# Gate columns of the Fourier and pooling branches as seven block products for eight, in the first mixing stage

## The reference, cut to what matters

```
h = rmsnorm(x, g_mix[l])
p = h @ w_in[l]                       # 1024 -> 512 F, 512 B, 512 C, 512 V, 512 P, 3 * 1024 gates
gates = sigmoid(p[..., OFF_G:])       # 0: Fourier, 1: convolution, 2: pooling
y_f = fourier_mix(p[F], w_fourier[l])           # FFT over tokens and channels, 128 x 256 maps
y_c = short_conv(p[B], p[C], p[V], w_conv[l], w_conv_out[l])
y_p = pool_mix(p[P], w_pool[l], pool_scale[l])
merged = gates0 * y_f + gates1 * y_c + gates2 * y_p
x = x + merged @ w_o[l]
```

## Time and profile before

| | before |
|---|---|
| median of three runs | 2216.32 us |
| profiled execution's own time | 2219.73 us |
| its span, first to last instruction | 2217.9 us |
| TensorE busy | 2208.1 us |
| VectorE busy | 1729.5 us |
| ScalarE busy | 1320.1 us |
| mean granted TensorE clock | 0.999 |

### The profile page before, as it was taken

How to read it: one execution, slowest core, us unless ns; L and a number is a source line. 1 busy time by engine, 2 the same in 40 slices (tenths; PEclk the granted TensorE clock), 3 DMA queues, 4 the chain that set the end, 5 groups by cost and what they waited for, 6 DMA issues and landing times.

```text
span 2217.9 us, 28791 instructions
## 1 busy us (share of the span) xinstructions
PE 2208.1 (100%) x11494; PEld 1886.3 (85%) x11494; DVE 1729.5 (78%) x2163; ACT 1320.1 (60%) x1489; POOL 56.2 (3%) x68
## 2 busy tenths in 40 slices
PE   9999999999999999999999999999999999999999
PEld 8888888888888888888888888888888888788887
DVE  7787566888788566788887799768788887976787
ACT  6565445556556544666656676555565667754554
POOL 0000000000000000000000000000000000000000
PEclk9999999999999999999999999999999999999999
DMA  8987555977879555698597753549778785345876
GB/s 278 312 233 260 166 186 188 311 224 232 287 245 275 182 173 207 221 300 234 193 319 232 238 171 113 203 162 326 229 235 277 239 259 196 107 162 195 283 247 185
DMA packets 170950, 503.86 MB, mean 227 GB/s; under 512 B 18720, under 2 KB 23328, under 8 KB 162624
## 3 DMA queue, kind: packets, MB, share of 16 engines
q1 hardware_dynamic: 161456, 434.90, 55.1%
q0 software_dynamic: 9216, 67.11, 15.5%
q10 hardware_dynamic: 144, 0.00, 0.0%
HBM read 500.91 MB, written 1.05 MB: 226 GB/s over the span
## 4 chain that ended last, share of the span: by engine, by line
PE 94%; DVE 2%; DMA 2%; ACT 1%; issue 0%; SPq 0%; ACTq 0%; DVEq 0%
PE psum L756 25%; PE psum L757 13%; PE psum L692 12%; PE psum L694 12%; PE psum L693 12%; PE psum L887 4%; PE psum L891 4%; PE psum L889 4%; PE psum L724 2%; PE psum L767 1%; DMA raw<-t_gate_up_1a_dram 1%; DVE split_w L1842 1%; PE psum L1114 1%; PE psum L775 1%; DMA raw<-w_a_alone_dram 0%
## 5 line engine op out<-in xcount | busy, mean ns | idle before, releaser
L1842 DVE TENSOR_TENSOR split_w<-raw,split_w 128x2048 fp32r<-128x2048 f32 (+3 forms) x389 | 842.5, 2177 | 149.1 <-ACT split_w L1314 146.8
L1314 ACT ACTIVATE split_w<-raw 128x2048 fp32r<-128x2048 f32 (+3 forms) x389 | 708.0, 1829 | 290.9 <-PE psum L694 61.8
L756 PE MATMUL psum<-xt,split_w 128*128 128x512 f32 x2464 | 860.1, 393 | 2.5 <-DVE xt L1864 2.5
L757 PE MATMUL psum<-xt,split_w 128*128 128x256 f32 x2464 | 689.8, 280 | 0.0
L756 PEld LDWEIGHTS psum<-xt,split_w 128*128 128x128 f32 x2464 | 462.0, 187 | 105.8 <-DVE xt L1864 2.8
L757 PEld LDWEIGHTS psum<-xt,split_w 128*128 128x128 f32 x2464 | 466.1, 189 | 0.5
L692 PE MATMUL psum<-split_w,xt 128*128 128x512 f32 (+1 forms) x736 | 289.5, 393 | 0.0
L694 PE MATMUL psum<-split_w,xt 128*128 128x512 f32 (+1 forms) x736 | 283.7, 385 | 0.0
L693 PE MATMUL psum<-split_w,xt 128*128 128x512 f32 (+1 forms) x736 | 283.6, 385 | 0.0
L1980 DVE TENSOR_TENSOR gate_up<-psum,low 128x512 f32<-128x512 f32 x176 | 120.8, 686 | 99.4 <-ACT low L1391 99.3
L692 PEld LDWEIGHTS psum<-split_w,xt 128*128 128x128 f32 x736 | 138.4, 188 | 29.0 <-issue 3.0
(11 more groups left out here) (309 smaller groups left out, 2870.8 us busy)
## 6 DMA issues: line engine op xcount, KB each, us to landing
raw<-w_in_dram SPq DMA_DIRECT2D x180, 512.0 KB, 4.5
raw<-t_gate_up_1b_dram SPq DMA_DIRECT2D x88, 512.0 KB, 6.4
raw<-t_gate_up_2a_dram SPq DMA_DIRECT2D x88, 512.0 KB, 6.1
raw<-t_gate_up_2b_dram SPq DMA_DIRECT2D x88, 512.0 KB, 6.1
raw<-t_gate_up_1a_dram SPq DMA_DIRECT2D x84, 512.0 KB, 6.9
left_sums<-ffn_w_down_quarters_dram POOLq DMA_DIRECT2D x24, 1024.0 KB, 10.4
raw<-ffn_w_down_quarters_dram SPq DMA_DIRECT2D x48, 512.0 KB, 4.3
left_sums<-w_a_quarters_dram POOLq DMA_DIRECT2D x12, 1024.0 KB, 10.8
```

Source lines behind the costliest of these rows:

```text
L756: nc.tensor.matmul(bank, whi[:, slot, w], xt[:, c, :, :], start=c == 0, stop=False)
L757: last = nc.tensor.matmul(bank[:, 0:T], wlo[:, slot, w], xt_hi[:, c, :], start=False, stop=c == DC - 1)
L1314: nc.scalar.activation(whi[:, e.unit(u) % HL, 0:n], raw[:, r, 0:n], ACT.Copy).then_inc(hi_done, 1)
L1842: nc.vector.tensor_tensor(wlo[:, e.unit(u) % HL, 0:n], raw[:, r, 0:n], whi[:, e.unit(u) % HL, 0:n], ALU.subtract).then_inc(w_ready, 1)
```

## The change

With the tokens in halves, the rows of k in odd and even chunks and the two branches' 512 columns as the two column blocks, the gate columns of the Fourier and the pooling branch of one n are one 2 x 2 by 2 x 2 block product. Eight block products (four units of 24 matmuls, 96 in all) become seven (seven units of 12, 84 in all), in the order "11", "U", "T2", "21", "T3", "22", "T4". Three of them ("11", "21", "22") take quarters as they are loaded from `w_in`, four take sums of quarters; the sums are made by VectorE, in `gate_left` (U = 11 + 12, then + 22, then + 21) and in place in the slot of "12" (T3 = 12 + 22). The load of "22" waits for U; the next unit's load waits for T4. A turn is now 12 units for 9: seven products, f (the Fourier map), p (the pooling map), two units of convolution gates, here c0 and c1, and co (`w_conv_out`). The stage has 38 units for 32.

TensorE collects "11", "T2", "T3", "T4" in one bank and "U", "22" in another; ScalarE copies the intermediate contents out to `sigs` (`snapshot`) before the next product is added, and VectorE adds or subtracts (`x00`, `x11`, `x01`) before the Sigmoids. The sums of the tokens' halves are made once a stage by VectorE (`token_sums`, `token_sums_lo`) and ScalarE. Some work changes place in VectorE's order: the convolution (`convolved`) now stands behind the split of c0, and `bz_rounded` behind the split of co.

```diff
+GATES = (10, 22)
+GATE_ORDER = ("11", "U", "T2", "21", "T3", "22", "T4")
+GATE_SUMS = {GATES[n] + GATE_ORDER.index(name): (n, name) for n in range(2) for name in ("U", "T2", "T4")}
+MIX_UNITS = {1: 38, 2: 36}
...
 # SyncE's queue
+                    for name, q in (("11", "11"), ("21", "21"), ("T3", "12")):
+                        gate_load(u0 + gate_unit(n, name), q, n)
+                    eng.wait_ge(gate_sums, 4 * gate_turn(e, n) + 1)
+                    gate_load(u0 + gate_unit(n, "22"), "22", n)
+                    eng.wait_ge(gate_sums, 4 * gate_turn(e, n) + 4)
...
 # TensorE
+                    product(n, "11")
+                    if n == 0:
+                        eng.wait_ge(acted, e.after(acted, ("tok", "B")))
+                        eng.wait_ge(acted, e.after(acted, ("zt", 1)))
+                        turns("bt", tok)
+                        eng.wait_ge(done, e.after(done, ("s",)))
+                    product(n, "U")
+                    eng.wait_ge(acted, e.after(acted, ("e1", n)))
+                    product(n, "T2")
+                    if n == 1:
+                        eng.wait_ge(acted, e.after(acted, ("sig", 0, "c")))
+                    product(n, "21")
+                    eng.wait_ge(acted, e.after(acted, ("e2", n)))
+                    product(n, "T3")
+                    eng.wait_ge(acted, e.after(acted, ("u", n)))
+                    product(n, "22")
+                    eng.wait_ge(acted, e.after(acted, ("e3", n)))
+                    product(n, "T4")
...
 # ScalarE
+                gate_sum_split(0, "U")
...
+                gate_sum_split(0, "T2")
+                to_sbuf(("tok", "B"), tok, 2, u0 + 9)
                 split(u0 + 13)
...
+                    snapshot("e1", "11", sigs[:, 0, 0, :])
+                    gate_sum_split(n, "T3")
+                    snapshot("u", "U", sigs[:, 1, 1, :])
+                    split(u + 5)
+                    snapshot("e2", "T2", sigs[:, 1, 0, :])
+                    gate_sum_split(n, "T4")
+                    eng.wait_ge(done, e.after(done, ("wf", n)))
+                    split(u + 7)
+                    snapshot("e3", "T3", sigs[:, 0, 1, :])
...
 # VectorE (after z; before, split(u0 + 10) stood ahead of z)
+                split(u0 + 10)
+                gate_sum(0, "U")
+                gate_sum_split(0, "U")
+                gate_sum(0, "T2")
+                gate_sum(0, "T3")
+                gate_sum_split(0, "T2")
+                gate_sum(0, "T4")
+                split(u0 + 13)
+                for n in range(2):
+                    split(u + 4)
+                    split(u + 5)
+                    x00; gate_sum_split(n, "T4"); fourier_weights(n); split(u + 7); x11; split(u + 8); x01
+                    split(u + 9)
+                    if n == 0:
+                        convolved()
+                    else:
+                        for j in range(2):
+                            turned_lo(mt1_hi, mt1_lo, ("mt0", j), 6 + j, 2 * j)
+                    merge(0, "f", 4, sigs[:, 0, :, :])
+                    split(u + 10)
+                    merge(1, "p", 2 * (1 - n), sigs[:, 1, :, :])
+                    split(u + 11)
+                    if n == 0:
+                        bz_rounded()
+                    split(u + 12)
+                    if n == 0:
+                        gate_sum(1, "U"); gate_sum_split(1, "U"); gate_sum(1, "T2"); gate_sum(1, "T3")
+                        gate_sum_split(1, "T2"); gate_sum(1, "T4")
+                    else:
+                        split(u + 13)
+                    merge(2, "c", 4, sig1)
+                    split(u + (15 if n == 0 else 14))
```

More of the change, by code:

```diff
@@ L404, in build @@
         taken = semaphore("taken")
+        gate_sums = semaphore("gate_sums")
         small = signal("small")
@@ L552, in ffn_loads, with gate_load @@
                         down_load(u0 + 2 * FG + i, part, w2)
+            def gate_load(u, q, n):
+                load(u, [(chunked(1024 * j, 2, 512), gate_quarter(e, q, n, j)) for j in range(2)])
             def mix1_loads(u0):
@@ L993, in mix1_tensor @@
                 turns("zt", z)
[L994 to L1026, removed]
@@ L1027, in mix1_tensor, with left, product @@
-                u += 3
-                eng.wait_ge(acted, e.after(acted, ("sig", 1, "f")))
-                wide(u, 0, XT)
+                wide(u, 2, XT, 1, 4)
+                def left(name, i):
+                    if name in SUMMED:
+                        return [w[:, i, SUMMED[name], :] for w in (s_hi, s_lo)]
+                    c, m = {"11": (2 * i + 1, 0), "21": (2 * i, 0), "T4": (2 * i, 1)}[name]
+                    return [w[:, c, m * P:(m + 1) * P] for w in XT]
+                def product(n, name):
+                    out = psum[:, bank_of(n, name), :]
+                    u = u0 + gate_unit(n, name)
+                    slot = e.unit(u) % HL
+                    eng.wait_ge(w_ready, units(e, u, RAW))
+                    for i in range(DC // 2):
+                        hi, lo = left(name, i)
+                        w = slice(i * 512, (i + 1) * 512)
+                        start = i == 0 and name in ("11", "U", "21")
+                        stop = i == DC // 2 - 1
+                        nc.tensor.matmul(out, hi, whi[:, slot, w], start=start, stop=False, skip_group_check=True)
+                        nc.tensor.matmul(out, hi, wlo[:, slot, w], start=False, stop=False, skip_group_check=True)
+                        last = nc.tensor.matmul(out, lo, whi[:, slot, w], start=False, stop=stop, skip_group_check=True)
+                    last.then_inc(w_used, 1)
@@ L1030, in mix1_tensor @@
+                u = u0 + GATES[1] + 12
+                eng.wait_ge(done, e.after(done, ("mt0", 1)))
                 eng.wait_ge(done, e.after(done, ("merged", 1, "p")))
[L1031 to L1035, removed]
                 wide(u, 0, MERGED, 0, 1)
@@ L1539, in mix1_scalar @@
-                split(u0 + 14)
-                s = 12
-                for n in range(2):
[L1542 to L1561, removed]
@@ L2208, in mix1_vector @@
[L2208 to L2213, removed]
-                                                  psum[:, 6 + j, :].rearrange("p (c t) -> p c t", c=2),
-                                                  cv[:, 2 * j:2 * j + 2, :], ALU.mult).then_inc(
-                                                      done, e.mark(done, ("bc", j)))
@@ L2257, in mix1_vector @@
-                        s += 3
+                    split(u + 4)
+                    split(u + 5)
+                    multiplied(u + 3)
+                    eng.wait_ge(acted, e.after(acted, ("e1", n)))
+                    nc.vector.tensor_tensor(sigs[:, 0, 0, :], psum[:, bank_of(n, "21"), :], sigs[:, 0, 0, :],
+                                            ALU.add).then_inc(done, e.mark(done, ("x00", n)))
+                    gate_sum_split(n, "T4")
+                    fourier_weights(n)
+                    split(u + 7)
@@ new lines, in mix1_vector @@
+                    eng.wait_ge(acted, e.after(acted, ("e3", n)))
+                    nc.vector.tensor_tensor(sigs[:, 1, 1, :], sigs[:, 1, 1, :], sigs[:, 0, 1, :],
+                                            ALU.subtract).then_inc(done, e.mark(done, ("x11", n)))
+                    split(u + 8)
+                    multiplied(u + 5)
+                    nc.vector.tensor_tensor(sigs[:, 1, 0, :], psum[:, bank_of(n, "22"), :], sigs[:, 1, 0, :],
+                                            ALU.subtract).then_inc(done, e.mark(done, ("x01", n)))
@@ new lines, in mix1_vector @@
+                    split(u + 9)
+                    if n == 0:
+                        convolved()
+                    else:
+                        for j in range(2):
+                            turned_lo(mt1_hi, mt1_lo, ("mt0", j), 6 + j, 2 * j)
+                    multiplied(u + 7)
+                    eng.wait_ge(acted, e.after(acted, ("sig", n, "f")))
+                    merge(0, "f", 4, sigs[:, 0, :, :])
+                    split(u + 10)
+                    multiplied(u + 8)
+                    eng.wait_ge(acted, e.after(acted, ("sig", n, "p")))
```

275 lines of the change are left out of this document (198 added, 77 removed).

## The result

The changed kernel takes 2268.64 us (median of four runs, 2267.92 to 2269.33), the kernel before 2216.7 (2216.0 to 2217.28): 1.0231 times as long, interval 1.0218 to 1.0244.

The account below looks back on a forecast made before the run. TensorE was taken to bound the kernel before, VectorE's work and order the changed stretch. 2216.3 + 40.2 for two layers' stalls + 0.8 for the clock = 2257.3 us (forecast chance 0.78), range 2240 to 2270.

Parts of the forecast that it names:

- TensorE's saving: Mixing stages: 12 matmuls fewer per turn, 24 per layer at 0.227 us, 5.45 us a layer, 10.9 in two.
- A sum takes 2.29 us: VectorE's 128 x 2048 weight sums: priced like a split, 2.21 us behind another, 2.29 to the semaphore; eight per layer, 17.7.
- The token sums: Stage's start: about 4.9 us and later 2.2 on VectorE, 1.8 on ScalarE, costed at nothing; uncovered, up to 7 us.
- a load lands 4.75 us after the first issue: Weight loads in the mixing turns: one landing time for all; 3.8 us makes it 17.5 a layer, 5.5 us 23.1.
- The clock: TensorE's slow stretches after gaps longer than 2.5 us: 0.4 us a layer added, bounds 0 and 5.
- The chain's 20.1: VectorE's order followed from z to `w_o`: stalls 24.5, less 5.45, plus restarts, 20.1 us later per layer.
- The upper end of the forecast's own range: Whole kernel: loads landing in 5.5 us with the clock's upper bound, 2271 us.
- the list of what would show it: Expected profile signs: TensorE waits 20 to 25 us per layer behind VectorE's low parts, longest 4 to 5; `w_o` 20 later.
- VectorE's busy share: Sign in the first layer's stretch: VectorE busy over 85% from 243 to 357 us.
- Rival B: Mixing stretch: VectorE's throughput alone counts, 15.9 us of idle times don't arise, 4.2 a layer, 2225 us; chance 0.09.
- Rival A: Mixing stretch: VectorE's added work all hidden, TensorE alone counts, 2205.4 us, faster; chance 0.04.
- Rival C: Mixing stretch: TensorE's clock stays at its lower level until `w_o`, 16 to 55 us more a layer, 2290 to 2365; chance 0.05.

Follow-up runs that it names:

- the convolution's place: Changed kernel with the convolution moved on VectorE from ahead of merge f and c1's split to behind them, first turn: 2268.3 us, 1.0227 of the kernel before.
- mt0's 3.4 per layer: Changed kernel with `mt0`'s low halves moved on VectorE from ahead of merge f to behind c1's split, second turn: 2259.1 us.
- B's copy: Changed kernel with `mt0`'s low halves behind c1's split and, on ScalarE, the `tok` copy ahead of T2's copy in the first turn: 2257.7 us.
- the experiment: Changed kernel with loads of gate quarters, c0, c1 and co cut to 128 of each 512 columns: 2253.6 us, 1.0163 of the kernel before.

## Why the prediction was right, and where its size was off

**Right.** TensorE's saving (48 matmuls) and the mechanism: the low parts of U, T2, "21", c0 and c1 come late since VectorE has more work in the stretch than TensorE leaves time for. A sum takes 2.29 us to its semaphore, as taken. The token sums are hidden. By hand the low part of c1 began 43.6 us after z and its memsets; in the trace it is 284.72 - 239.85 = 44.9. The same chain, followed again before the experiments, foretold that the convolution's place is worth nothing, mt0's 3.4 per layer (measured 4.9 and 6.1), and B's copy next to nothing. That the time lies inside the range is in part luck: the size was 11 us short, both terms that were too small erred the same way, and 1.4 us more would have been outside.

**The loads, mis-sized.** The term "a load lands 4.75 us after the first issue" was too small. Loads with no other beside them took 5.15 and 5.17, c1's 5.2, and co's, issued 1.2 us behind c1's, 7.1. The range that I gave to this term (3.8 to 5.5) held the first three and not the last. The chain had one number for every load, from a median of the old order, where `w_conv_out` took 4.1. How much of the 5.2 and 5.6 us missing per layer this is, lies between the 3 of the rows and the 4 to 5 of the experiment.

**The clock, slightly mis-sized.** 0.4 us a layer was forecast, 1.0 and 2.4 measured, inside the bounds of 0 and 5. Not foreseen was that a gap of 2 us can be enough: the clock fell behind 1.96 us at U of the first layer. It is no fixed length, for it stayed at its upper level behind 2.11 us at the second layer's U, and behind 2.60 us in the kernel with sums of 64 columns. The gap and the clock behind it (2 us from 306 and from 862), first and second layer:

```profile
305.36 0.50 PE L1048 MATMUL psum<-split_w,mt_hi 128*128 128x512 f32 x1 [1.96 <-DVE split_w L1962]
...
860.60 0.50 PE L1048 MATMUL psum<-split_w,mt_hi 128*128 128x512 f32 x1 [2.11 <-DVE split_w L1962]
```
```profile
306.00:308.00 2.00, 2.00 (x6) 1.59 (x5) 1.77 (x1) 0.00 (x0) 0.00 (x0) 0.50 0.00 0
...
862.00:864.00 2.00, 1.66 (x8) 1.01 (x6) 2.00 (x2) 0.34 (x1) 0.00 (x0) 1.00 0.00 0
```

In all the clock is at its lower level for a quarter of the stretch in the first layer and a fifth in the second (1 - 0.88 = 0.12 and 1 - 0.90 = 0.10, twice that). That so much slow time costs so little was argued rightly: it ends in the next wait. The chain's 20.1, 3 to 5 for the loads and 1.0 to 2.4 for the clock make 24 to 27.5 for the 25.7 and 26.1 measured. Some 0.9 us by which the low part of c1 came late (44.9 for 43.6 above, less 0.4 for the load) is in none of these terms.

**A sum.** The upper end of the forecast's own range, 2271, comes out of its terms as 2216.3 + 2 x (23.1 + 5) = 2272.5; nothing else rests on it.

**Waits of TensorE, in the list of what would show it.** 20 to 25 us per layer were expected and 18.1 and 20.4 found, as slow products stand in place of some. In the first layer c1 of the first turn (4.03 for 4.2) and U (1.96 for 1.8) fit; T2 and "21" of the second turn are 3.1 and 3.0 for 4.4 and 4.5, with U and T2 run at the lower clock ahead of them. In the second layer, where U ran at the upper level, T2's is 4.52. c1 of the second turn has 3.1 and 3.7 for 2.2. The stalls at co (2.3 and 1.0) and at T4 (0.3 and 0.9) are not there, but for 0.7 at co of the second layer's first turn: the product ahead of co, c1, ran half slow and ended that much later.

**VectorE's busy share fell short:** over 85% was expected from 243 to 357 us, 91.6 / 114 = 80% found. The 85% was the sum's 97.2 us in a stretch of 94 + 20; the stretch grew to 120, and 97.2 / 120 is 81%. Rival B (throughput alone, 2225) needed the chain's 15.9 us of idle time not to arise, and the loads and ScalarE's copies added to it: what costs is each wait of VectorE in its order, on top of its work. Rival A fell with the first wait. Rival C fell with the changed kernel's own clock, which came back to its upper level after each wait, 0.88 and 0.90 over the stretch.

## What to carry to other kernels

Before taking work from an engine that never waits, add up what the edit gives to the engine behind it, stretch by stretch, and then walk that engine's order: the sum says whether it can pay, the order says how much is lost. A wait that is taken away from one unit is worth nothing where the same work still stands ahead of the next; moving work past another engine's handoff is worth the idle time. Price a load by whether others are issued beside it in the new order, not by its median in the old one.

## What the runs showed of the hardware

While GpSimd adds two tiles of SBUF, a VectorE operation with two operands in SBUF hardly moves: 6.36 us for 2.29, beside a sum of 4.58 with which it overlaps for 4.2. TensorE's clock fell from its upper to its lower level behind one gap of 1.96 us and not behind others of 2.11 and 2.60, came back after some 3 to 6 us of work, and cost 1 to 2 us per stage where TensorE wasn't the bound, though the loss read from the clock alone was 11 to 14.
